# Moving the transposes of the picks' scores and the first gate groups two blocks later, and giving four of the last eight up blocks to ScalarE's queue

## The reference

```python
def peer(h, w_q, sub_keys, w_down, w_up):
    q = (ht @ w_q).reshape(T, PEER_HEADS, 2, PEER_HALF_DIM)
    scores = jnp.einsum('thic,hikc->thik', q, sub_keys)
    sv, si = lax.top_k(scores, PEER_TOPK)
    cand = sv[:, :, 0, :, None] + sv[:, :, 1, None, :]
    best, ci = lax.top_k(cand.reshape(T, PEER_HEADS, -1), PEER_TOPK)
    i1 = jnp.take_along_axis(si[:, :, 0], ci // PEER_TOPK, axis=-1)
    i2 = jnp.take_along_axis(si[:, :, 1], ci % PEER_TOPK, axis=-1)
    expert = i1 * PEER_N_KEYS + i2
    gate = jax.nn.softmax(best, axis=-1)
    hid = jax.nn.gelu(jnp.einsum('cd,ckd->ck', xb, w_down[eb]))
    return jnp.einsum('ck,ckd->cd', gb * hid, w_up[eb])
```

## Time and profile before

| | us |
|---|---|
| median of 3 runs (1530.65, 1532.68, 1533.99) | 1532.68 |
| span of the profiled execution | 1534.2 |
| PE busy | 1488.9 (97%) |
| DVE busy | 889.9 (58%) |
| POOL busy | 715.3 (47%) |
| ACT busy | 476.7 (31%) |
| DMA engines, mean over the span | 341 GB/s |

### The profile page before, as it was taken

How to read it: one execution, slowest core, us unless ns; L and a number is a source line. 1 busy time by engine, 2 the same in 40 slices (tenths; PEclk the granted TensorE clock), 3 DMA queues, 4 the chain that set the end, 5 groups by cost and what they waited for, 6 DMA issues and landing times.

```text
span 1534.2 us, 29704 instructions
## 1 busy us (share of the span) xinstructions
PE 1488.9 (97%) x10668; PEld 1448.4 (94%) x10668; DVE 889.9 (58%) x2900; ACT 476.7 (31%) x1199; POOL 715.3 (47%) x632
## 2 busy tenths in 40 slices
PE   7999999999999999999999999999899999999995
PEld 6789999999999999999977999999899999999995
DVE  1740899857886344444723349996588933444363
ACT  5654331228881000001055532221688500000001
POOL 6567023348995222233467731233699832223250
PEclk9999999999999999999999999999999999999998
DMA  6455899999999999999954468999999999999992
GB/s 236 145 178 169 292 353 407 407 387 341 385 384 402 409 409 410 410 409 409 364 192 152 158 222 318 406 408 409 347 373 384 386 409 409 410 409 410 410 409 112
DMA packets 144993, 523.13 MB, mean 341 GB/s; under 512 B 17008, under 2 KB 17264, under 8 KB 144496
## 3 DMA queue, kind: packets, MB, share of 16 engines
q1 hardware_dynamic: 67696, 240.62, 41.8%
q0 software_dynamic: 55296, 201.35, 33.5%
q10 hardware_dynamic: 21888, 79.70, 13.0%
HBM read 519.48 MB, written 1.05 MB: 339 GB/s over the span
## 4 chain that ended last, share of the span: by engine, by line
PE 72%; DMA 12%; DVE 9%; issue 3%; ACT 2%; POOL 1%; SPq 0%; DVEq 0%; POOLq 0%; ACTq 0%
PE ps L943 71%; DMA arena<-in_rows,ret 9%; DVE arena L1561 2%; DVE arena L1508 2%; DMA spare<-in_wu 2%; DVE oh_buf L1476 1%; DVE oh_buf L1473 1%; DVE arena L1480 1%; DMA raw<-in_wm 1%; PE ps L951 1%; ACT arena L632 1%; POOL arena L574 1%; POOL w_lo L557 1%; ACT hT_hi L659 1%; DVE ret L1476 0%
## 5 line engine op out<-in xcount | busy, mean ns | idle before, releaser
L943 PE MATMUL ps<-arena,w_raw 128*128 128x160 f32 (+1 forms) x2944 | 418.1, 301 | 2.7 <-issue 2.6
L943 PE MATMUL ps<-arena,raw 128*128 128x160 f32 (+1 forms) x2944 | 412.9, 299 | 0.2
L943 PEld LDWEIGHTS ps<-arena,w_raw 128*128 128x128 f32 x2944 | 406.8, 191 | 4.5 <-issue 4.3
L943 PEld LDWEIGHTS ps<-arena,raw 128*128 128x128 f32 x2944 | 403.2, 190 | 1.6 <-issue 1.6
L574 POOL DMA_INDIRECT arena<-in_wu,ret x192 | 187.8, 978 | 365.5 <-DVE oh_buf L1625 275.7
L574 POOL DMA_INDIRECT arena<-in_rows,ret x192 | 200.3, 1043 | 302.3 <-ACT ret L832 104.5
L1625 DVE SCALAR_TENSOR_TENSOR oh_buf<-arena,ret,oh_buf 128x1024 f32<-128x1024 f32 x126 | 161.8, 1285 | 241.2 <-DMA arena<-in_wu,ret 241.1
L557 POOL TENSOR_TENSOR w_lo<-raw,w_hi 128x1024 fp32r<-128x1024 f32 x80 | 193.1, 2423 | 95.2 <-PE ps L943 65.8
L1508 DVE SCALAR_TENSOR_TENSOR arena<-arena,ps 128x1024 f32<-128x1024 f32 x128 | 153.7, 1214 | 0.0
L922 ACT ACTIVATE arena<-ident 128x768 f32<-128x768 f32 x2 | 1.7, 842 | 448.7 <-PE ps L943 448.7
L810 ACT ACTIVATE arena<-ps 128x160 f32<-128x160 f32 x160 | 48.4, 303 | 270.7 <-PE ps L943 248.7
(11 more groups left out here) (144 smaller groups left out, 1784.6 us busy)
## 6 DMA issues: line engine op xcount, KB each, us to landing
raw<-in_wd SPq DMA_DIRECT2D x108, 512.0 KB
w_raw<-in_wd SPq DMA_DIRECT2D x108, 512.0 KB
raw<-in_wm SPq DMA_DIRECT2D x80, 512.0 KB
raw<-in_wu ACTq DMA_DIRECT2D x28, 512.0 KB
raw<-in_wu SPq DMA_DIRECT2D x28, 512.0 KB
w_raw<-in_wu SPq DMA_DIRECT2D x28, 512.0 KB
w_raw<-in_wu ACTq DMA_DIRECT2D x28, 512.0 KB
low_rows<-in_wu SPq DMA_DIRECT2D x22, 512.0 KB
```

The costliest lines, as they stand in the source:

```text
L943: return nc.tensor.matmul(out, lhsT, rhs, start=start, stop=stop, skip_group_check=shared)
```

## The change

The transposes and the wait before them move from before block 77 to before block 79. Gate groups start at block 82, not 80; blocks 80 and 81 are therefore written straight by ACT, so DVE has two multiplications fewer, and ACT writes fewer ones. The dot products that DVE takes after the early ones end at the same block as before and are spread over two blocks fewer (42 for 44). Of the last eight up blocks in each layer, those in slots 1, 3, 5 and 7 are issued by ACT, behind its write of zeros to `upT` and ahead of the next layer's `high_part`.

```diff
-IDS_AT = 77
+IDS_AT = 79
...
-G_FROM = 80
+G_FROM = 82
...
-    return EARLY + max(0, min(ROWS - EARLY, (b - G_FROM - 1) * (ROWS - EARLY) // 44))
+    return EARLY + max(0, min(ROWS - EARLY, (b - G_FROM - 1) * (ROWS - EARLY) // 42))
...
-                for j in range(UP_RAW // 2):
+                for j in range(0, UP_RAW // 2, 2):
                     sp.wait_ge(w_used, (l + 1) * LAYER - UP_RAW + j + 1)
                     load_up(LAST_FROM + j, j)
...
                                      scale=0.0).then_inc(upT_zero, 1)
+                for j in range(1, UP_RAW // 2, 2):
+                    act.wait_ge(w_used, (l + 1) * LAYER - UP_RAW + j + 1)
+                    nc.scalar.dma_start(up_raw[j], wu_d[l, LAST_FROM + j]).then_inc(up_full[j], 16)
                 if l + 1 < LAYERS:
```

## The result

The change makes the kernel slower: median 1545.8 us (1542.04 to 1548.37, 4 runs) against 1533.3 us of the kernel before beside it (1530.65 to 1538.2, 4 runs). The ratio is 1.0063, 95% interval [1.0043, 1.0082], where 0.995 was forecast. The profiled span is 1543.0 us, 8.8 longer than before's 1534.2.

A forecast was written before the change was run, and what follows sets the result against it. PE, busy 97% of the span, was taken as the bound, so only its waits could be won. Down stages 2.1, layer 0's up stage 0 and layer 1's 5.66 make 7.8 us off: 1524.9 us, range 1520.5 to 1531.

The forecast's parts named there:

- the sum of the down stages: Both layers' down stages: charges less 4.35 us give -1.35 us in layer 0, -0.75 in layer 1, together 2.1 won.
- (a): First gate: POOL's first one-hots come late, costing 0.3 us in layer 0 and 0.9 in layer 1.
- (b): Gates: POOL gets 11 rounds of two gathers for 9, making PE wait about 2.3 us per layer.
- Part 1: Down stages: transposes and gates two blocks later remove the waits for DVE's picks; 2.1 us won over both layers.
- (c): Behind the last gate: seven dot products in six blocks' time, one more bank read late, 0.4 us.
- Part 2: End of up stages: four blocks through ACT's queue end both stalls; layer 0 wins nothing, layer 1 5.66 us.
- Rival 2: End of up stages: the second queue brings nothing, only 2.1 us remain, 1530.6 us; chance 0.16.
- rival 4: First gates: the last gathers stay slow, POOL's first one-hots come 4.8 us later per layer, 1536.3 us; chance 0.06.
- Rival 1: Layer 0's gathers don't lag (2.24 us), and charges (a) and (b) halve (about 2.5): 1520.5 us; chance 0.14.

The follow-up runs named there:

- two blocks sooner: Kernel before with transposes before block 75, gates from block 78, dot products over 46 blocks, last up blocks on SP's queue: 1.0021.
- Part 1 alone: Kernel before with transposes and gates two blocks later and spread 42 for 44, all up blocks on SP's queue: 1540.7 us, 1.0044.
- before again: Kernel before, unchanged, run once more for a second profile: 1532.5 us, 0.9999.
- dot products two groups sooner: Kernel before with transposes and gates two blocks later, dot products of the gates started two groups sooner over 46 blocks: 1.0008.
- the second series: Both kernels run again without edit: before 1532.5 us, changed kernel 1537.9 us, 1.0035.
- the first series: First measurement, 4 runs each: changed kernel 1545.8 us against 1533.3 us of the kernel before, 1.0063.
- the two kernels with earlier dot products: Dot products two groups sooner over 46 blocks, against before: with transposes and gates two blocks later 1.0008; with ACT's queue and POOL's low parts held 0.9947.
- held low parts: Kernel before with ACT's queue in both layers and POOL's low parts held until DVE's sums are done: 1531.5 us, 0.9971.
- all of it two blocks sooner: Kernel before with transposes before block 75, gates from 78, spread 46, ACT's queue in both layers, POOL's low parts held: 1.0024.

## Why the prediction was wrong

**The step that failed** is the sum of the down stages: "six blocks follow instead of eight: 2 x 2.18 = 4.35 us less". The blocks do move, 18.64 to 14.29 us with the spread unchanged. But they move ahead of the gates, and there they were to fill waits of 2.74 and 3.91 us that the six other profiles with the old place don't have. The 10 us that two stalls "cost with their clocks" were one execution's place for time that PE loses anyway: 186 us up to the first gate with the wait at the transposes and without it. Of the 5.3 and 3.8 us by which the first row of the table grew, 4.35 are the two blocks. Without them it is 186.9 and 185.6 us for before's 186.0 and 186.1, and over all profiles 183.0 to 186.9 with the new place and 184.1 to 187.4 with the old one: a scatter of 3 to 4 us that no edit explains. The move alone shows the sum: 324.7 us from the first down to the first up block for 324.9, so nothing of the 4.35 us per layer comes off the time.

An example of that scatter: the window over ten us early in the down stage, block 23 or so, first before and then after:

```profile
208.00:218.00 10.00, 8.72 (x55) 7.32 (x54) 7.34 (x69) 3.93 (x14) 5.04 (x6) 1.00 1.02 408
```

```profile
208.00:218.00 10.00, 5.89 (x22) 5.09 (x22) 5.74 (x55) 2.39 (x9) 3.52 (x4) 0.76 1.02 409
```

22 products for 55, with pauses of 4.3 us in all without a releaser (1.25 before), and a clock of 0.76. After's second profile needs 188.7 and 187.3 us for this row, not 191.3 and 189.9.

**(a) POOL's first one-hots**: 0.3 and 0.9 us late were forecast, nothing was seen, since PE comes later. They are the bound when the gates start sooner (two blocks sooner: waits of 1.61 and 2.98 us).

**(b) POOL in the gates**: the mechanism was right, the size wrong. Six waits of 0.2 to 0.3 us, at every third group, made the rounds about 2.5 us longer in all (2.3 forecast); the other 2.1 us come from the last two builds, 2.53 and 2.58 us for 1.59. The prediction named the contention of two SBUF inputs for the long sum of layer 0 and did not ask which dot products the denser spread brings beside POOL's last builds. The term measured 4.66 us per layer, and with 4.35 us not coming off it is what made the kernel slower: the spread alone has 1.0035, the whole of Part 1 1.0044 [1.0028, 1.0060], and with 44 put back the changed kernel has 1.0000.

**(c) the dot products behind the last gate**: 0.4 us forecast, 0.38 measured (14.67 for 14.29).

**What no term held**: bytes, though they are no part of this kernel's loss. The prediction did not ask for Part 1 what the transfers do when the last dot product moves. In the move alone it moves two blocks, and the kernel loses 0.31%, 4.7 us, of which 3.5 us are seen in layer 0's up stage. The changed kernel avoids that by its spread of 42: its last dot product belongs to block 125 as before, eight gathers are issued before the up stage, and 121.2 and 121.0 MB are moved by then (121.3 and 121.0 before). So the costs of the move alone (1.0031) and of the spread alone (1.0035) don't add up to Part 1's 1.0044.

**Part 2**: layer 0 gained nothing, by the wait that was foreseen (2.4 us forecast, 2.37 seen). In layer 1 the wait for the last block is gone, but 5.66 us were priced by the longest wait of all profiles, with its clock; where the queue is SP's alone the others have 2.16 (before again), 1.97 (Part 1 alone), 2.35 (move alone), 2.27 (dot products two groups sooner), 1.40 (two blocks sooner) and none (spread alone). Alone, the queue is worth 0.18%, 2.8 us. Rival 2, that it brings nothing, is excluded, if narrowly.

The forecast was on the wrong side, and no rival covers it: rival 4 has the sign, but its mechanism is absent. (Rival 1's own terms, 7.8 + 2.24 + 2.5, give 1520.1 and not 1520.5; nothing hangs on it.) Added up by what was measured: 0.44% for move and spread together, less 0.18% for the queue, is 1.0026; the second series has 1.0035 [1.0023, 1.0048].

**Open**: why the first series has 1.0063 and the second 1.0035; the two intervals touch only at 1.0043 to 1.0048. What lets PE pause in single products with no releaser. Why the queue in layer 1 alone is not better than in both. By what the two kernels with earlier dot products gained, since the bytes that they were built for did not move.

## What to carry to other kernels

A wait seen in one profile is a place where lost time showed, not yet an amount to win: take a second profile, and compare the length of the whole stretch before pricing its removal. Where a later stage runs at full transfer rate, transfers that are not issued before it begins are paid there, so count those that are (five gathers for eight) before looking at the engine with the waits. A window in which the DMA engines idle (193 GB/s for 288) is not yet such a debt: undo it, and see whether the later stage gets shorter. When work is made denser, check which operands the instructions that move now have beside the other engine's.

## What was not expected of the hardware

PE paused without a releaser in layer 1's last blocks in three profiles with the second queue (after, held low parts, all of it two blocks sooner), each time 1.5 to 2.1 us behind a packet of an instruction queue. (Two blocks sooner, without that queue, has one pause of 0.42 us there.) DMA queues of after from 1494 to 1495 us; the pauses follow from 1496.8 on:

```profile
q0 software_dynamic: 84, 0.32, 79.6%
q1 hardware_dynamic: 28, 0.09, 22.8%
q8 instruction: 1, 0.02, 6.1%
```

The packet comes near this place of the program in every profile looked at, mostly without a pause. In the microsecond of the packet POOL's queue had 65.1, 71.3 and 79.6% of the engines' time where PE paused, but 70.2% in before's first profile, 66.2% with Part 1 alone and 65.4% with the queue in layer 1, where it did not, so this share does not tell the cases apart. That the pauses are late instructions is a guess that nothing here tests.
